# Attention B: values as three fp32r products of 256 columns, with probabilities and values split in two parts

## What is computed

```python
kvb = (ckv_all @ lw['w_kvb']).reshape(b, n_keys, H_B, NOPE_B + VD_B).transpose(0, 2, 1, 3)
kb_nope = rmsnorm(kvb[..., :NOPE_B], lw['mla_kn_nope'])
vb = kvb[..., NOPE_B:]                       # values, 128 wide
...
def one_block(q_blk):
    sc = jnp.einsum('bkgqd,bksd->bkgqs', q_blk, k).astype(jnp.float32) * scale
    p = jax.nn.softmax(sc, axis=-1).astype(v.dtype)
    return jnp.einsum('bkgqs,bksd->bkgqd', p, v)
```

## Time and profile before

| | |
|---|---|
| median of 3 runs | 1747.09 us |
| profiled execution: its time, its span | 1747.53 us, 1745.7 us |
| TensorE busy over the span | 1552.4 us, 89% |
| VectorE, ScalarE, GpSimd busy | 1014.4, 728.9, 646.4 us |
| mean granted clock | 0.964 |
| attention B in the trace | 341.7 to 500.7 us |
| TensorE, VectorE, ScalarE, GpSimd busy in it | 143.2, 104.8, 62.3, 40.1 us |

### The profile page before, as it was taken

How to read it: one execution, slowest core, us unless ns; L and a number is a source line. 1 busy time by engine, 2 the same in 40 slices (tenths; PEclk the granted TensorE clock), 3 DMA queues, 4 the chain that set the end, 5 groups by cost and what they waited for, 6 DMA issues and landing times. The chain is left out here.

```text
span 1745.7 us, 22717 instructions
## 1 busy us (share of the span) xinstructions
PE 1552.4 (89%) x7699; PEld 1172.1 (67%) x7699; DVE 1014.4 (58%) x1578; ACT 728.9 (42%) x1067; POOL 646.4 (37%) x727
## 2 busy tenths in 40 slices
PE   7799787898989999999892999999999999999990
PEld 2688687788889999954532766666666666666660
DVE  1966687666674475535632655555555555555544
ACT  2523343334331231112112665555565656655650
POOL 0535364422223332300073454444444444444430
PEclk9999999999999999999896999999999999999996
DMA  9320100000034475362444999999999999999944
GB/s 321 98 95 3 37 1 1 1 1 2 19 109 132 130 239 145 96 234 68 186 165 139 337 367 361 349 342 342 352 356 349 336 342 345 337 337 339 339 139 183
DMA packets 129672, 352.50 MB, mean 202 GB/s; under 512 B 21316, under 2 KB 77256, under 8 KB 102600
## 3 DMA queue, kind: packets, MB, share of 16 engines
q1 hardware_dynamic: 97880, 237.71, 37.3%
q10 hardware_dynamic: 10288, 71.86, 11.0%
q0 software_dynamic: 21440, 42.08, 9.6%
HBM read 335.16 MB, written 47.87 MB: 219 GB/s over the span
## 5 line engine op out<-in xcount | busy, mean ns | idle before, releaser
L2259 DVE TENSOR_TENSOR e_wlo<-mem,e_whi 128x2048 fp32r<-128x2048 f32 x140 | 314.6, 2289 | 110.7 <-ACT e_whi L2199 110.7
L2199 ACT ACTIVATE e_whi<-mem 128x2048 fp32r<-128x2048 f32 x140 | 260.2, 1911 | 29.4 <-PEq L1859 24.5
L2169 PE MATMUL psum<-mem 128*128 128x512 f32 x560 | 252.0, 593 | 1.5 <-ACT mem L2231 1.5
L2149 PE MATMUL psum<-e_whi,e_xhi 128*128 128x512 f32 x560 | 228.6, 408 | 7.1 <-DVE e_xlo L2266 7.1
L2106 POOL TENSOR_TENSOR held<-nhalf 1x1 f32<-1x1 f32 x206 | 119.6, 580 | 287.4 <-DMA sums<-mem,si 116.9
L2150 PE MATMUL psum<-e_whi,e_xlo 128*128 128x512 f32 x560 | 222.5, 397 | 0.0
L2151 PE MATMUL psum<-e_wlo,e_xhi 128*128 128x512 f32 x560 | 222.5, 397 | 0.0
L2169 PEld LDWEIGHTS psum<-mem 128*128 128x128 f32 x560 | 101.0, 190 | 102.2 <-issue 102.1
L1493 POOL TENSOR_TENSOR w_lo<-mem,w_hi 128x1024 fp32r<-128x1024 f32 x30 | 76.9, 2584 | 161.0 <-ACT w_hi L1437 161.0
L2266 DVE TENSOR_TENSOR e_xlo<-psum,e_xhi 128x512 fp32r<-128x512 f32 x140 | 90.2, 686 | 77.7 <-ACT e_xhi L2205 77.7
L2276 DVE TENSOR_TENSOR mem<-mem,psum 128x256 f32<-128x256 f32 x70 | 42.6, 608 | 157.1 <-ACT mem L2238 157.1
(11 more groups left out here) (317 smaller groups left out, 3321.3 us busy)
## 6 DMA issues: line engine op xcount, KB each, us to landing
mem<-in_w_e SPq DMA_DIRECT2D x144, 1024.0 KB, 12.1
mem<-in_w_e ACTq DMA_DIRECT2D x66, 1024.0 KB, 11.2
mem<-in_w_mod SPq DMA_DIRECT2D x24, 1024.0 KB, 12.0
mem<-in_w_in SPq DMA_DIRECT2D x16, 512.0 KB, 4.5
mem<-in_w_in SPq DMA_DIRECT2D x3, 2048.0 KB, 8.9
sums<-mem SPq DMA_DIRECT2D x10, 512.0 KB, 17.0
mem<-sums SPq DMA_DIRECT2D x10, 512.0 KB, 7.6
mem<-in_x_sample SPq DMA_DIRECT2D x8, 512.0 KB, 11.5
```

The lines of the kernel that those rows point to most:

```text
L2149: pe.matmul(out, xh, wh, start=first, stop=False)
L2169: mm = pe.matmul(pY[:, cs], gT[:, f, :], w2[v][:, f, cs], start=(f == 0), stop=(f == 1))
L2199: act.activation(wHi13[u % 2][:, a], w13[u][:, a], ACT.Copy).then_inc(se["h13"], 1)
L2259: dve.tensor_tensor(wLo13[u][:, a], w13[u][:, a], wHi13[u % 2][:, a].bitcast(F32), ALU.subtract)\
```

## The change

For B alone:

- ScalarE's `take_p` copies all five transposed blocks into `pt_hi` (fp32r, the high part), and stands before `softmax(n)` in a round, not after it.
- VectorE's `take_p` waits for that copy and writes the remainder `pt_lo` (five blocks, PSUM less `pt_hi`), where it copied four blocks.
- GpSimd splits each head's values: `values_split(h)`, two copies to `vb_hi` and two subtractions to `vb_lo`. It follows `power(h + 1)`; from the second head on it waits until the head before has finished its value products.
- TensorE multiplies values for pairs of query tiles, in the rounds in which `values` of tiles 2 and 4 stood: for each of five key tiles three fp32r products of 256 columns. `values` of tiles 1 and 3 only keep their wait. In a round `values(n - 2)` now stands before `turn_p(n - 1)`.

The context tile's product is as it was.

```diff
@@ turn_p, values (TensorE) @@
                         pe.wait_ge(s["TeV"], n)
-                        if n >= 2:
+                        if n >= 2 and not mla:
                             pe.wait_ge(s["TeA"], late(n - 1))
...
+                def pair_values(h, t):
+
+                    if t % 2:
+                        return
+                    if t == 2:
+                        pe.wait_ge(s["vl"], 2 * (h + 1))
+                        if h:
+                            pe.wait_ge(s["Oe"], h)
+                    out = pO[:, (t - 2) * P:t * P]
+                    for j, kt in enumerate(KEY_TILES):
+                        vh = vh4[:, j, :] if j < 4 else vh1[:, :]
+                        pe.matmul(out, vh, pTh[:, j, :], start=(j == 0), stop=False)
+                        pe.matmul(out, vh, pTl[:, j, :], start=False, stop=False)
+                        mm = pe.matmul(out, vLo[:, kt, h, :], pTh[:, j, :], start=False, stop=(j == 4))
+                    if t == NT - 1:
+                        mm.then_inc(s["O"], 1)
...
+                    if mla and n > lag:
+                        values(n - lag - 1)
                     if lag <= n < N + lag:
                         turn_p(n - lag)
-                    if n > lag:
+                    if not mla and n > lag:
                         values(n - lag - 1)
@@ take_p and the loop (ScalarE) @@
+                    if mla:
+                        c = (t - 1) % 2 * P
+                        act.activation(pTh[:, :, c:c + P], pT_ps[:, 0:640].rearrange("p (j q) -> p j q", j=5), ACT.Copy)\
+                           .then_inc(s["TeA"], 1)
+                        return
...
-                    if not mla and lag <= n < N + lag and TILES[n - lag][1]:
+                    if lag <= n < N + lag and TILES[n - lag][1]:
                         take_p(n - lag)
                     if n < N:
                         softmax(n)
-                    if mla and lag <= n < N + lag and TILES[n - lag][1]:
-                        take_p(n - lag)
@@ GpSimd @@
+                    def values_split(h):
+
+                        if h:
+                            pool.wait_ge(s["O"], h)
+                        pool.tensor_copy(vh4[:, :, :], vB[:, 1:5, h, :]).then_inc(s["vh"], 1)
+                        pool.tensor_copy(vh1[:, :], vB[:, 5, h, :]).then_inc(s["vh"], 1)
+                        pool.wait_ge(s["vh"], 2 * h + 2)
+                        pool.tensor_tensor(vLo[:, 1:5, h, :], vB[:, 1:5, h, :], vh4[:, :, :].bitcast(F32), ALU.subtract)\
+                            .then_inc(s["vl"], 1)
+                        pool.tensor_tensor(vLo[:, 5, h, :], vB[:, 5, h, :], vh1[:, :].bitcast(F32), ALU.subtract)\
+                            .then_inc(s["vl"], 1)
...
                         power(h)
+                        values_split(h - 1)
+                    values_split(nh - 1)
@@ take_p (VectorE) @@
+                    elif mla:
+                        c = (t - 1) % 2 * P
+                        dve.wait_ge(s["TeA"], late(n))
+                        dve.tensor_tensor(pTl[:, :, c:c + P], pT_ps[:, 0:640].rearrange("p (j q) -> p j q", j=5),
+                                          pTh[:, :, c:c + P].bitcast(F32), ALU.subtract).then_inc(s["TeV"], 1)
```

More of the change, by code:

```diff
@@ L755, in attend @@
         pTc = mem.at(at[-1] + 2560, P)
+        if mla:
+            pTh, pTl = fp32r("pt_hi", at[-1], 5, 2 * P), fp32r("pt_lo", at[-1] + 1280, 5, 2 * P)
+            vh4, vh1 = fp32r("vb_hi4", M_SC + 8000, 4, P), fp32r("vb_hi1", M_SC + 4096, P)
+            vLo = fp32r("vb_lo", M_R + 6144, NK, HB, VD)
         names = ("S", "nm", "exp", "ri", "pn", "T", "TeV", "TeA", "O", "Oe", "C", "Ce") + (
-            ("Z", "qc", "sq", "ss", "ms", "rs", "iv", "q", "QT", "qe", "ql", "kh", "kl", "mx") if mla else
+            ("Z", "qc", "sq", "ss", "ms", "rs", "iv", "q", "QT", "qe", "ql", "kh", "kl", "mx", "vh", "vl") if mla else
             ("qh", "ql", "rp", "rc", "rq", "rd", "rm", "rr", "rx", "ws"))
@@ L883, in values @@
                         pe.matmul(pC, v[:, 0, :], pTc, start=True, stop=True).then_inc(s["C"], 1)
+                        return
+                    if mla:
+                        pair_values(h, t)
                         return
```

## The result

| | before | after |
|---|---|---|
| median | 1747.1 us (1747.0 to 1749.0, 4 runs) | 1786.9 us (1785.4 to 1790.3, 4 runs) |
| ratio, 95% interval | | 1.0227, 1.0211 to 1.0243 |
| profiled execution: its time, its span | 1747.5, 1745.7 us | 1790.3, 1788.4 us |
| mean granted clock | 0.964 | 0.953 |
| attention B in the trace | 341.7 to 500.7 us | 343.9 to 544.0 us |

The change costs 39.8 us in the medians; the forecast was 1784, a loss of 37. In the profiled executions, 42.7 us apart in span, attention B is 41.1 us longer, the stages ahead of it (the same code) 2.2 us, and what comes after it takes 1244.4 us where it took 1245.0. So all of the loss is in the stage that was changed, and I divide it by heads.

What follows compares the result with a forecast made beforehand. It took a nearly closed loop, scores to maximum to exponential to scores, under TensorE's pace as the bound: 1747.1 + 26.7 (six heads 20.0, plus first and last) + 10 for the clock = 1784 us, range 1767 to 1797.

Steps and rivals of the forecast that it cites:

- 1 to 2: Tile 1's scores to tile 2's: values, then VectorE's query remainder delay the scores; 4.82 us, was 3.90, +0.92.
- 2 to 3: Tile 2's scores to tile 3's: nothing of the change falls here, 0; was 2.23 us.
- 3 to 4: Tile 3's scores to tile 4's: tile 2's exponential starts later and VectorE's chain follows; +0.3 us, was 5.25.
- 4 to 0: Tile 4's scores to next head's tile 0: values and copy now precede the exponential; 5.69 us, was 3.94, +1.75, main term.
- 0 to 1: Tile 0's scores to tile 1's: transposes and the 640-column copy precede the exponential; 4.34 us, was 3.97, +0.37.
- The product: TensorE's fp32r value product of 256 columns: 0.118 us each, 1.77 a pair, saving 0.47 a pair.
- rival 2: Attention B, faster: splits stay hidden and TensorE's shorter program bounds; 1740 us, chance 4%.
- nine falls at 1.2 us: TensorE's granted clock in attention B: about one fall a head to 1.2 GHz, +10 us (ends 0 and +15).
- the two places that the prediction named: Thin TensorE spots: transposes, a 1.8 us wait, five short products; and tile 3 to 4, between waits of 0.8, 0.45, 1.3.
- Taken at 0: GpSimd's value split, about 2.3 us a head, might hold VectorE's small product: ends 0 and +1.2 a head, 0 taken.
- rival 3: Dearer: 256-column products cost like 320 ones, or GpSimd holds VectorE's small product every head; 1793 to 1803 us, chance 10%.
- the first and the last head: Attention B's ends: first head +2.05 us; last +1.4 for four steps and +3.2 for its serial drain.

Runs made afterwards that it cites:

- e5: Kernel after, with only tile 4's round back in the old order (transposes before values, exponential before copy, normalisation before VectorE's take): 1779.5 us, ratio 1.0127.
- e3: Kernel before, its fp32 values kept, with values moved ahead of the transposes and ScalarE's 128-column copy ahead of the exponential in attention B: 1762.9 us, ratio 1.0088.
- e2: Kernel after, plus unread products in TensorE's waits, eleven ahead of tile 0's scores and eight ahead of tile 4's: 1777.2 us, ratio 1.0169.
- e9: Kernel after, plus two GpSimd two-input additions ahead of each head's value split, results overwritten: 1813.8 us, ratio 1.0317.
- e1: Kernel after, making only the five high by high products of each pair's fifteen, copies and waits kept: 1780.3 us, ratio 1.0188.
- e10: Kernel after with only the five high by high products a pair, plus unread products ahead of tile 0's and tile 4's scores: 1773.2 us, ratio 1.0091.
- e8: Kernel after, old order in tile 4's and 0's rounds, query remainder first in tile 1's, nine unread products ahead of tile 4's scores: 1768.2 us, ratio 1.0058.

## Why the prediction was right

**The bound and the chain.** The five steps, worked out and measured in the head at full clock: 1 to 2, 4.82 and 4.91; 2 to 3, 2.23 and 2.23; 3 to 4, 5.55 and 5.56; 4 to 0, 5.69 and 5.82; 0 to 1, 4.34 and 4.32. Sum 22.6 and 22.84. The reading of the earlier trace rows that carried it was that the loop from scores over the exponential to scores is nearly closed, so that work ahead of the exponential counts in full and work beside it counts for nothing. e5 undid the largest step alone, e3 made two of them in the old kernel without any of the new arithmetic.

**The product.** 0.118 was taken, 0.12 measured (432.94 to 434.73 for fifteen, 1.79 against 1.77 a pair). TensorE's busy time of a head fell by 0.38, for the forecast's 0.94 (two savings of 0.47); where the rest of it went I did not follow, as TensorE no longer bounds. Nobody gained from it, as rival 2 would have needed.

**The clock.** Forecast were nine falls at 1.2 us, +10. In the six heads they cost 8.5 us (145.5 less 6 x 22.84), in five of them, in pieces of 1.3 to 1.5, 2.8 in the last of these; e2 gave back 10 us in the whole. All five lie in step 4 to 0, behind the second of the two places that the prediction named; behind the first, the wait of 1.75 ahead of tile 0, the clock held. The step was right in size, but that is partly luck: it rested on one stretch alone, and fewer falls at a higher price each made the sum. What the trace still doesn't say is when the clock falls. Tile 3's step and the 4 us behind it, in a head with a fall and in one without, kernel after:

```profile
377.41:382.97 5.56, 3.22 (x24) 2.51 (x21) 4.57 (x11) 3.50 (x8) 2.09 (x4) 0.98 0.00 0
382.97:386.97 4.00, 4.00 (x19) 4.00 (x20) 2.42 (x5) 0.51 (x1) 0.85 (x2) 0.60 0.00 0
425.81:431.37 5.56, 3.22 (x24) 2.51 (x22) 4.57 (x11) 3.47 (x8) 2.11 (x4) 1.00 0.00 0
431.37:435.37 4.00, 4.00 (x30) 3.83 (x30) 2.50 (x5) 0.54 (x1) 2.12 (x2) 1.00 0.00 0
```

TensorE did the same in both, busy 3.22 of 5.56 us; once it is at 1.2 GHz behind that, once at 2.4. The waits make the fall possible, and what decides in one head I can't show.
The Trainium skill, "TensorE: Matmul & The Clock Gate", section "What's actually happening", has the engine go back to its slow clock after a spell in which it was idle. The longest waits of TensorE in these heads are 1.8 us, with work on both sides; so that section's rule explains neither the falls here nor that e2 removes them.

**GpSimd.** Taken at 0, and right: in the trace of the kernel after, the split's instructions lengthened none of the small products by more than 0.03 us. The long ones of the stage stand beside other work of GpSimd. In the first head it is the keys' remainder (1.04 us, before 1.60), in the last what the earlier trace rows showed, the weights of the next stage:

```profile
525.65 1.99 DVE L1148 TENSOR_TENSOR small<-small 128x1 f32<-128x1 f32 x1
```

The kernel before had both, so they are no part of the loss. e9 shows that rival 3 had its mechanism but not its place.

**Mis-sized: the first and the last head.** The first took +1.6, for +2.05, and the chain in it cost more than that: its steps 3 to 4 and 4 to 0 grew by 0.6 and 1.9 us (5.03 to 5.61, 3.94 to 5.82). The clock hid 0.9 of it, by chance: the other three steps have the same work in both, and took 3.66, 4.09 and 3.75 us at a granted clock of 0.61, 0.92 and 0.56 before, 4.41, 3.98 and 2.22 at 0.50, 0.96 and 1.00 after. The last took +9.6, for the 4.6 of the chain and its share of the falls. In e2, whose last 30 us are at a clock of 0.89 in the mean (before 0.93), it is 6.5 above the kernel before, so about 6 is the serial drain (4.6 was too little by some 2) and about 3 is the clock, 0.74 in the change. The split is read from one run each and is rough.

The sum: chain of six heads 20.0, measured 21.2; first 2.05 and 2.5; last 4.6 and about 6.5; clock 10 and about 11 (8.5 and 3.1, less 0.9 in the first head). 36.7 against 40.9 in the stage of the profiled execution, which was the slowest of the four, and 39.8 in the medians.

## What to carry to other kernels

Where one engine's queue holds both the step that releases the bottleneck and a copy that waits for the bottleneck's later work, the order of the two is worth more than the arithmetic that is saved: with the values first in both, the copy behind the exponential cost 0.3 us a head, ahead of it 2.1. Price a change to a tile loop by the chain from one tile to the next, once for each kind of tile, and ask of every moved instruction who stands behind it in its queue. And when an edit opens waits or takes work off TensorE, read the granted clock head by head before believing either a gain or a loss.

## What the runs showed of the hardware that I had not expected

Taking work away from TensorE gave back less than half of what it should, since the clock fell more often: ten products fewer a pair (e1) left most heads at 0.86 in the mean and 23.8 us, and the same kernel with nineteen unread products a head (e10) took 20.73. Unread products of 256 columns in waits of about 1.2 to 1.8 us removed all the falls in six heads, in three kernels out of three (e2, e8, e10), and with more work the six heads were 8 to 16 us shorter each time (145.5 to 137.2, 126.1 to 117.8, 139.9 to 124.4). VectorE's product of one column took 0.16 us. Where it started inside a GpSimd instruction with more than 0.17 us still to run, it ended within 0.03 us behind that instruction, in all 68 such cases of attention B in the eleven traces (0.26 and 0.38 us in e9, 1.99 beside one of 2.34), and no product was long without one. So the price of the meeting is the rest of GpSimd's instruction. A product that starts first pays nothing: the one at 426.18, 0.11 us ahead of the subtraction, took 0.16.
